# Attention scores in two matmuls instead of three and four, and a shifted order of the softmax steps on ScalarE and VectorE

## The reference

```python
# first block, heads 0-7: window of 128; 4 query heads share one of 2 key heads
s = einsum('bnqhgd,bnkhd->bnhgqk', qb, kk) * ATTN_SCALE      # then + bias, mask, softmax with a sink
# first block, heads 8-15: the two 256-token blocks, which comes to causal attention
s_own = einsum('bhqd,bhkd->bhqk', q_c, k_own) * ATTN_SCALE   # then + bias, mask, softmax
# second block, 16 heads, causal, with forget gates (F is a running sum of log_sigmoid over the tokens)
logits = einsum("bhqd,bhkd->bhqk", qb, kb) + F[q] - F[k]     # then mask, softmax
```

## Time and profile before

| | us |
|---|---|
| median of 3 runs (2031.15 to 2031.51) | 2031.24 |
| the profiled execution, device time | 2031.23 |
| its span in the profile | 2029.4 |
| first attention stage (first score at 75.8) | 73 to 245 |
| second attention stage (first score at 1406.0) | 1405 to 1591 |
| TensorE busy in the span | 1954.0 |

### The profile page before, as it was taken

One profiled execution on the slowest core, in us unless ns is written; L12 is line 12 of the kernel. 1 busy time (PEld: TensorE's weight loads), 2 busy tenths in 40 slices (PEclk: granted clock), 3 DMA queues, 4 the chain that ended last, 5 costly groups with the idle time before them and its releaser, 6 DMA issues.

```text
span 2029.4 us, 22573 instructions
## 1 busy us (share of the span) xinstructions
PE 1954.0 (96%) x9134; PEld 1607.5 (79%) x9134; DVE 1163.7 (57%) x1841; ACT 757.0 (37%) x1141; POOL 333.2 (16%) x293
## 2 busy tenths in 40 slices
PE   4999999999999999999999999999999899999997
PEld 3888888778888887887888888868888678888885
DVE  6566565576676745666655654565666554432445
ACT  4556632352223234223422122374565352222223
POOL 4422211021111102003100000147222130000002
PEclk9999999999999999999999999999999999999998
DMA  9422366266565424432654523232111122323321
GB/s 330 138 82 63 114 232 236 83 219 215 210 219 196 166 85 169 161 108 80 237 195 169 187 87 100 86 123 88 43 42 43 64 91 95 104 83 104 98 90 42
DMA packets 126121, 267.57 MB, mean 132 GB/s; under 512 B 4463, under 2 KB 33151, under 8 KB 126016
## 3 DMA queue, kind: packets, MB, share of 16 engines
q1 hardware_dynamic: 121056, 248.59, 35.9%
q0 software_dynamic: 4960, 17.53, 2.4%
HBM read 261.84 MB, written 8.45 MB: 133 GB/s over the span
## 4 chain that ended last, share of the span: by engine, by line
PE 66%; ACT 5%; DVE 4%; POOL 2%; issue 1%; DMA 1%; ACTq 0%; SPq 0%; DVEq 0%; POOLq 0%
PE ps L599 21%; PE ps L601 21%; PE ps L600 21%; DVE t L1629 1%; ACT t L1164 1%; ACT t L1160 1%; ACT t L1206 1%; ACT t L1118 1%; PE ps L756 1%; POOL t L2227 1%; DVE t L1663 1%; DVE t L1601 0%; DVE t L1554 0%; DMA x_keep<-t 0%; POOL t L2042 0%
## 5 line engine op out<-in xcount | busy, mean ns | idle before, releaser
L599 PE MATMUL ps<-t 128*128 128x512 f32 (+1 forms) x2504 | 969.5, 387 | 17.5 <-DVE t L1629 4.3
L601 PE MATMUL ps<-t 128*128 128x512 f32 (+1 forms) x2504 | 962.8, 385 | 0.0
L600 PE MATMUL ps<-t 128*128 128x512 f32 (+1 forms) x2504 | 962.0, 384 | 0.0
L599 PEld LDWEIGHTS ps<-t 128*128 128x128 f32 x2504 | 471.4, 188 | 119.0 <-DVE t L1494 6.5
L1494 DVE TENSOR_TENSOR t<-t 128x2048 fp32r<-128x2048 f32 x133 | 305.0, 2294 | 441.9 <-ACT t L1111 441.9
L601 PEld LDWEIGHTS ps<-t 128*128 128x128 f32 x2504 | 470.9, 188 | 98.9
L600 PEld LDWEIGHTS ps<-t 128*128 128x128 f32 x2504 | 471.2, 188 | 94.2 <-issue 1.0
L1111 ACT ACTIVATE t<-t 128x2048 fp32r<-128x2048 f32 x133 | 254.3, 1912 | 618.6 <-PE ps L601 611.1
L1554 DVE SCALAR_TENSOR_TENSOR t<-ps,t 128x512 f32<-128x512 f32 x184 | 132.6, 748 | 91.5 <-PE ps L601 82.7
L1506 DVE CUSTOM_DVE_ANT_0 t<-t 128x1024 f32<-128x1024 f32 x144 | 175.5, 1260 | 10.3 <-DMA t<-in_ada_t 3.6
L1629 DVE TENSOR_TENSOR t<-ps,t 64x512 fp32r<-64x512 f32 (+4 forms) x183 | 103.8, 577 | 103.4 <-ACT t L1238 48.7
(11 more groups left out here) (170 smaller groups left out, 1561.8 us busy)
## 6 DMA issues: line engine op xcount, KB each, us to landing
t<-in_ada SPq DMA_DIRECT2D x48, 1024.0 KB, 6.0
t<-in_gate SPq DMA_DIRECT2D x22, 1024.0 KB, 5.0
t<-in_up SPq DMA_DIRECT2D x22, 1024.0 KB, 5.1
t<-in_down SPq DMA_DIRECT2D x22, 1024.0 KB, 5.1
t<-in_w_in SPq DMA_DIRECT2D x17, 1024.0 KB, 5.7
t<-in_w_mlp_in SPq DMA_DIRECT2D x16, 1024.0 KB, 5.4
t<-in_w_mlp_out SPq DMA_DIRECT2D x16, 1024.0 KB, 5.1
t<-in_ada_t POOLq DMA_DIRECT2D x13, 1024.0 KB, 6.0
```

The source lines that it names most:

```text
L599: pe.matmul(o, wh, xh, start=first, stop=False)
L600: pe.matmul(o, wh, xl, start=False, stop=False)
L601: return pe.matmul(o, wl, xh, start=False, stop=last)
```

## The change

It has four parts.

1. **Scores in two matmuls.** Each head gets a full tile of 128 rows: its own 64 rows hold q-high, the other 64 hold q-low (`halves_of_queries`). The key high tile holds k-high twice, in both halves of the rows; one matmul then gives q-high by k-high and q-low by k-high. The second matmul takes the key tile with k-low in the head's own rows. In stage 1 its other rows are zero. In stage 2 they hold the ones and the forget sums (`gate_places`), and the moving side is `QF`: q-high in the head's own rows, the masked forget rows in the others. So a tile is two matmuls of the same shape in both stages, in place of three and four.
2. **Evacuation in halves.** A query tile leaves as two 64 x 512 copies on ScalarE and two 64 x 512 operations on VectorE. A key head leaves as two ScalarE copies (own rows and other rows) and one low half; the shared window keys (`ka`) with two low halves. Half of the zero memsets go (4 of 8 in stage 1 on GpSimd, 4 on VectorE and 4 on GpSimd in stage 2).
3. **Forget rows.** They are made on 32 partitions. VectorE has three more operations of 32 x 512, ScalarE three copies (one of 512, two of 1024 elements) in place of six, and GpSimd makes `QF` in two operations of 64 x 512 for each head where it had one of 128 x 512.
4. **Order.** `moved` shifts steps in an engine's own walk of the list: "score" steps are 2.5 places later on ScalarE and 2.5 sooner on VectorE, counted in the list with all engines' steps. In a causal head without evacuation VectorE now has: norm, t(h, 2), out(h-1), score 0, t(h, 3), score 1, t(h+1, 0), score 2, score 3, t(h+1, 1); ScalarE: norm, t(h, 2), out(h-1), t(h, 3), t(h+1, 0), score 0, score 1, t(h+1, 1), score 2, score 3. TensorE's and GpSimd's order stay.

The host no longer reorders the columns of `w_in` and rows of `w_branch_a`; shapes and bytes of the weight DMAs stay.

```diff
+def moved(steps, by):
+
+    return [step for _, step in sorted(enumerate(steps), key=lambda e: e[0] + by.get(e[1][0], 0))]
...
-            Qa = sb(outer, [2, 4, T], R)
-            Qb = sb(outer, [2, 4, T], R)
+            Qa = sb(outer, [8, T], R)
+            Qb = sb(outer, [8, T], R)
...
-            Q2 = sb(ph, [2, KT, T], R)
+            Q2 = sb(ph, [16, T], R)
             with ExitStack() as inner:
                 KVt = sb(inner, [12288], R)
                 pt2 = sb(inner, [2, 1280], R)
-                AFr = [sb(inner, [T], R) for _ in range(2)]
-                BF = sb(inner, [T], R)
+                QF = [sb(inner, [T], R) for _ in range(2)]
             with ExitStack() as top:
...
-                t, g = h % 4, h // 4
+                t, g = h // 2, h // 4
                 kv = KV1[0]
-                return dict(kind="swa", sink=small[:, h:h + 1], q=(Qa[:, 0, t, :], Qa[:, 1, t, :]), qt=("qa", t),
-                            k=(k_view(kv)[:, 0, g, :], k_view(kv)[:, 1, g, :]), kt=("ka", g), zero=0,
+                return dict(kind="swa", sink=small[:, h:h + 1], q=Qa[:, h, :], qt=("qa", t),
+                            out=(Qa[:, 2 * t, :], Qa[:, 2 * t + 1, :]),
+                            k=(k_view(kv)[:, 0, g, :], k_view(kv)[:, 1, 2 * g + h % 2, :]), kt=("ka", g), zero=0,
                             v=lambda j: (v_view(kv)[:, 0, j, 0:P], v_view(kv)[:, 1, j, 0:P]), vt=[("va", 0)],
-                            r0=64 * g, table=h, width=256)
+                            r0=64 * (h % 2), s0=64 * g, table=h, width=256)
             g, n = (h - 8) // 4, h % 4
...
-                if st == 1 and 4 <= h < 8:
-                    on.wait_ge(d_lo, "out", 1, h - 4)
-                if (st, hd["zero"]) == (2, 0):
-                    on.wait_ge(d_evac, "zero", 2, 0)
+                o = psum[bank][:, 0:N]
+                pe.matmul(o, hd["q"][:, tok], hd["k"][0][:, kr], start=True, stop=False)
+                q = hd["q"]
+                if st == 2:
+                    q = QF[h % 2]
+                    on.wait_ge(p_fox, "af", h)
+                    if hd["zero"]:
+                        on.wait_ge(p_fox, "bf", 1)
+                    else:
+                        on.wait_ge(a_gate, "bf", 0)
                 else:
-                    on.wait_ge(p_zero, "zero", st, hd["zero"])
-                o = psum[bank][:, 0:N]
-                pe.matmul(o, hd["q"][0][:, tok], hd["k"][0][:, kr], start=True, stop=False)
-                pe.matmul(o, hd["q"][1][:, tok], hd["k"][0][:, kr], start=False, stop=False)
-                ins = pe.matmul(o, hd["q"][0][:, tok], hd["k"][1][:, kr], start=False, stop=st == 1)
-                if st == 2:
-                    on.wait_ge(p_fox, "af", h)
-                    on.wait_ge(a_gate, "bf")
-                    ins = pe.matmul(o, AFr[h % 2][:, tok], BF[:, kr], start=False, stop=True)
-                ins.then_inc(mm.sem, mm.up("score", st, h, i))
+                    on.wait_ge(p_zero, "zero", 1, hd["zero"])
+                pe.matmul(o, q[:, tok], hd["k"][1][:, kr], start=False, stop=True).then_inc(mm.sem, mm.up("score", st, h, i))
                 freed[bank] = [(d_soft, ("top", st, h, i))]
 
...
-                on.wait_ge(a_gate, "fF")
-                on.wait_ge(d_fox, "lo")
+                on.wait_ge(d_fox, "sum rows")
...
+        own = [slice(0, 64), slice(64, 128)]
         def halves_of_keys(name, bank, i):
             kv = k_view(KV1[0] if name == "ka" else kv_of[name])
             for odd in range(2):
-                r, n = slice(64 * odd, 64 * odd + 64), 2 * i + odd
-                yield n, psum[bank][r, :], kv[r, 0, n, :], kv[r, 1, n, :]
+                n = 2 * i + odd
+                his = [kv[own[p], 0, n, :] for p in (odd, 1 - odd)]
+                if name == "ka":
+                    los = [(kv[own[p], 1, 2 * n + p, :], kv[own[p], 0, n, :]) for p in range(2)]
+                else:
+                    los = [(kv[own[odd], 1, n, :], his[0])]
+                yield n, psum[bank][own[odd], :], his, los
+        def halves_of_queries(name, t):
+            q = {"qa": Qa, "qb": Qb, "q2": Q2}[name]
+            for odd in range(2):
+                yield own[odd], q[own[odd], 2 * t + odd, :], q[own[1 - odd], 2 * t + odd, :]
...
-            for s in range(2):
-                for odd in range(2):
-                    r = slice(0, 64) if odd else slice(64, 128)
-                    yield k_view(kv)[r, s, odd::2, :].bitcast(F)
+            for odd in range(2):
+                yield k_view(kv)[own[1 - odd], 1, odd::2, :].bitcast(F)
+
+        def gate_places(kv):
+
+            for odd in range(2):
+                r = 64 * (1 - odd)
+                yield r, k_view(kv)[r:r + 32, 1, odd::2, :], k_view(kv)[r + 32:r + 64, 1, odd::2, :]
+
+        def twice(rows):
+
+            return rows.rearrange("p (a n) -> p a n", a=1).broadcast_to([32, 2, T])
...
-                act.activation(of_queries(name)[:, 0, t, :], psum[bank][:, :], ACT.Copy, scale=QSCALE).then_inc(
-                    a_hi.sem, a_hi.up(name, t))
+                for rows, hi, lo in halves_of_queries(name, t):
+                    ins = act.activation(hi, psum[bank][rows, :], ACT.Copy, scale=QSCALE)
+                ins.then_inc(a_hi.sem, a_hi.up(name, t))
 
             def keys(name, bank, n, i):
                 on.wait_ge(mm, "job", n, i)
-                for k, src, hi, lo in halves_of_keys(name, bank, i):
-                    act.activation(hi, src, ACT.Copy).then_inc(a_hi.sem, a_hi.up(name, k))
+                for k, src, his, los in halves_of_keys(name, bank, i):
+                    for hi in his:
+                        ins = act.activation(hi, src, ACT.Copy)
+                    ins.then_inc(a_hi.sem, a_hi.up(name, k))
 
...
-                for step in stage_steps[st]:
+                for step in moved(stage_steps[st], {"score": 2.5}):
...
-            act.activation(fhi[0:16, :], fr, ACT.Copy).then_inc(a_gate.sem, a_gate.up("fhi"))
-            on.wait_ge(a_gate, "fhi")
-            act.activation(fF, fhi[0:16, :].bitcast(F), ACT.Copy).then_inc(a_gate.sem, a_gate.up("fF"))
-            on.wait_ge(a_gate, "fF")
-            on.wait_ge(p_fox, "ones of AF")
-            on.wait_ge(p_fox, "ones of BF")
-            act.activation(AF[0:16, :], fF, ACT.Copy)
-            on.wait_ge(d_fox, "lo")
-            act.activation(AF[32:48, :], z3, ACT.Copy)
-            act.activation(BF[64:80, :], fF, ACT.Copy, scale=-1.0)
-            act.activation(BF[96:112, :], z3, ACT.Copy, scale=-1.0).then_inc(a_gate.sem, a_gate.up("bf"))
+            act.activation(fhi[0:32, :], fr, ACT.Copy).then_inc(a_gate.sem, a_gate.up("fhi"))
+            on.wait_ge(d_fox, "sum rows")
+            for r, one, gates in gate_places(KV2[0]):
+                ins = act.activation(gates, twice(AF[0:32, :]), ACT.Copy, scale=-1.0)
+            ins.then_inc(a_gate.sem, a_gate.up("bf", 0))
...
-                Q = of_queries(name)
                 on.wait_ge(a_hi, name, t)
-                dve.scalar_tensor_tensor(out=Q[:, 1, t, :], in0=psum[bank][:, :], scalar=QSCALE, in1=Q[:, 0, t, :].bitcast(F),
-                                         op0=ALU.mult, op1=ALU.subtract).then_inc(d_lo.sem, d_lo.up(name, t))
+                for rows, hi, lo in halves_of_queries(name, t):
+                    ins = dve.scalar_tensor_tensor(out=lo, in0=psum[bank][rows, :], scalar=QSCALE, in1=hi.bitcast(F),
+                                                   op0=ALU.mult, op1=ALU.subtract)
+                ins.then_inc(d_lo.sem, d_lo.up(name, t))
 
             def keys(name, bank, i):
-                for k, src, hi, lo in halves_of_keys(name, bank, i):
-                    low_half(lo, src, hi, name, k)
+                for k, src, his, los in halves_of_keys(name, bank, i):
+                    on.wait_ge(a_hi, name, k)
+                    for lo, hi in los:
+                        ins = dve.tensor_tensor(lo, src, hi.bitcast(F), ALU.subtract)
+                    ins.then_inc(d_lo.sem, d_lo.up(name, k))
...
-                for step in stage_steps[st]:
+                for step in moved(stage_steps[st], {"score": -2.5}):
...
-            for v in zero_places(KV2[0]):
-                ins = dve.memset(v, 0.0)
-            ins.then_inc(d_evac.sem, d_evac.up("zero", 2, 0))
...
-            dve.tensor_tensor(z3, fr, fhi[0:16, :].bitcast(F), ALU.subtract).then_inc(d_fox.sem, d_fox.up("lo"))
+            dve.tensor_tensor(z3, fr, fhi[0:32, :].bitcast(F), ALU.subtract).then_inc(d_fox.sem, d_fox.up("lo"))
+            on.wait_ge(d_fox, "lo")
+            dve.tensor_scalar(z3, z3, lower, 1.0, ALU.mult, ALU.mult).then_inc(d_fox.sem, d_fox.up("lower rows"))
+            on.wait_ge(d_fox, "lower rows")
+            on.wait_ge(p_fox, "ones of AF")
+            for r in (0, 64):
+                dve.scalar_tensor_tensor(out=AF[r:r + 32, :], in0=fhi[0:32, :].bitcast(F), scalar=upper, in1=z3, op0=ALU.mult,
```

(29 more changed lines are left out.)

86 lines of the change are left out of this document (44 added, 42 removed).

## The result

The changed kernel takes 2000.43 us (median of 4 runs) against 2031.2 us: ratio 0.9842, 95% interval 0.9828 to 0.9855, 30.8 us or 1.5% less. The prediction was 2003.3 us, range 1997 to 2012.

A forecast was written before the change was run, and what follows sets the result against it. TensorE, busy 1954.0 of 2029.4 us, was taken as the bound except in the last heads (ScalarE and VectorE). -8.9 + 1.1 - 18.1 + 0.8 - 5.0 + 2.2 = -27.9 us gave 2003.3 us, range 1997 to 2012.

The forecast's parts named there:

- A stretch where TensorE is the bound: -8.9: Stage 1: one score product fewer per tile in 8 window and 8 causal heads saves 8.9 us.
- -18.1: Stage 2 before the last heads: two of four score products go, 1.29 us a head in 14 heads.
- The last heads. Here it is the new order that counts: End of stage 2: the new order removes VectorE's two pauses, 9.6 to 7.1 us a head, saving 5.0 us.
- Rival B: Both stages: the order also removes TensorE's present idle time, 6 us more, 1994 to 1999 us; chance 0.15.
- Hidden by TensorE's projection units: Stage 1: added evacuation copies, 7.1 us of ScalarE and 2.8 of VectorE, cost nothing beside TensorE's work.
- Rival A: Middle of stage 2 or 1: softmax on ScalarE and VectorE becomes the bound, 2009 to 2018 us; chance 0.14.
- +0.8: Stage 2, three heads with a key result and four weight pieces: ScalarE's work exceeds TensorE's need, adding 0.8 us.
- +1.1: First query tiles of stage 1: four ScalarE copies delay a weight slot that TensorE waits for, by 1.1 us.
- +2.2: Start of stage 2: key copies and forget-row steps delay a weight slot TensorE needs by 2.2 us, bounds +1 and +3.5.
- C: Rival: GpSimd's added operation in each of 16 heads holds VectorE up, +11 us at most, halved 2009; chance 0.05.
- D: Rival: slower than before, VectorE standing before unmade score products while its delayed low half is needed, 2036 us; chance 0.02.
- E: Rival: the change alters nothing, because the removed score products were hidden; chance 0.01.

The follow-up runs named there:

- no_shift: The changed kernel with its two new mask columns put into unused columns of another small array, so no later array moves; 2008.7 us.
- fewer_products_new_order: The kernel before with only the new order, leaving out one score product in stage 1 and two in stage 2, evacuations as before; 1987.2 us.
- early_conversion: The changed kernel with ScalarE converting the next weight slot while it waits for the gate's sums at the start of stage 2; 1990.2 us.

## Why the prediction was right in its total and wrong in its account

Adding the medians, one part after the other, gives this account: order alone -19.5, products in the new order -24.9, evacuations and what goes with them +21.5, moved arrays -8.2; sum -31.1. The prediction had order -5.0, products -27.0, evacuations +4.1, arrays 0; sum -27.9. The steps depend on their sequence: with the products first they bring 5.6 us and not 24.9, and the order, last, 40.6.

**"A stretch where TensorE is the bound: -8.9", and "-18.1" in stage 2.** The size per product was right, 24.9 for 27.0 where TensorE does bind. The premise was wrong for the kernel before: there the omission brings 5.6. TensorE busy 165.8 of 172 us was read as bound by TensorE. But a busy share does not say that less work would end sooner: with the work removed the stage lost 0.6 us, and TensorE's idle time grew from 5.4 to 11.3. This was the step that failed first.

**"The last heads. Here it is the new order that counts", -5.0.** In the last heads it held: 6.81 and 7.57 us for 7.1. But the pause it describes, VectorE standing for ScalarE's copy behind an exponential, was in every head, and the prediction looked for it only where TensorE was visibly idle. Rival B named the place, at a chance of 0.15 and 6 us; the order is worth 19.5 alone and 40.6 with the new products.

**"Hidden by TensorE's projection units".** In stage 1 the added evacuations were costed at nothing, with a cover named by busy shares of 68 and 70%. They cost 6.8 us there, 6.5 of them ahead of the first causal head's fourth-tile exponential, so in the window heads; with the maxima alone moved 155.7 us remain against 152.6. In the old order they cost more: stage 1 is 175.3 us for the 166.5 with as many products and the old evacuations. A busy share says nothing of a queue in which each added copy lies between two handovers. Rival A's mechanism, softmax's engines as the bound, was thus at work, in stage 1, and the order kept it small. In stage 2 the +0.8 was too small as well. Of the 8.0 us there (no_shift against fewer_products_new_order) 3.2 lie ahead of the first fourth-tile exponential and 4.8 behind it; 1.1 of these are the last loop with its lower clock, and 3.7 the middle, which therefore does not hide its copies: TensorE's sums wait 5.6 us for low halves (L787) where they waited 2.2. The prediction's own sign, a softmax loop in the middle longer than 10.2 us, did come: three loops of stage 2 take 14.0 to 16.0 us. It was set badly, since the same three take 13.2 to 17.1 before and 12.9 to 14.1 without the new evacuations; over four heads of the middle the loops are 10.5 us on average for 10.1.

**First queries and start of stage 2.** +1.1 was +1.7 at the first score, and 1.4 at the wait it was read from (2.10 us where 0.74 stood). The slot at the start of stage 2 was to come 2.2 us later (2.26 by its working, which has 2.7 for VectorE in one place and adds 2.6) and came 2.3 later against the first score, so that chain was read well. But the wait at the start of stage 2 was to be 3 to 4 us and was 4.95, and the lower clock's 1.6 us behind it were in no term: the +2.2 measured 5.0: 3.4 of wait, of them 0.8 VectorE held up by GpSimd and 0.2 the two missing products, and 1.6. Of the later query tiles "hidden" was wrong for one: the forget gate's first product waits 2.92 us for VectorE (L1665), where it waited 1.55 before.

**Nothing in the sum for addresses.** The change adds two columns to a persistent array, and the text passed over them. 8.2 us, a quarter of the result.

**C, D, E.** C's price is refuted, while its collisions exist. D and E did not happen; but a time above the kernel before was nearer than 0.02 makes it, by another way than D's: without the order the same products end at 2041.0.

**The total.** The order brought 14.5 us more than its term, the evacuations cost 17.4 more, the products brought 2.1 less, and the moved arrays gave 8.2: four errors that come to 3.2 us. That the total lies in the range is luck.

## What to carry to other kernels

A nearly full engine is not a bound until less work on it shortens the stage: hold its idle time against what is to be saved, and follow two in-order engines that feed each other through one unit of the steady state, looking for "stands for the other" on both sides. Put the producer's step (here the maximum) ahead of anything in its queue that waits for the consumer; half of a reordering may do, and each stage can want its own. Judge a half by what its waits do to the engine that should be the bound, not by the idle time of the engine that you moved. Time a change of layout against a control in which only the addresses move.

## What the runs showed of the hardware that was not expected

Moving SBUF arrays by 8 or by 32 bytes a partition made the same kernel 9.0 and 10.1 us faster of 2031: where one triple of 512-column products in two took 0.70 us (0.2333 each), moved ones mostly take 0.69 or 0.68. Taking the 8 bytes back cost 8.2 us. The Trainium skill ("SBUF — State Buffer", section "SBUF: two separate sides") says that within the engine side only the port pair shared by VectorE and GpSimd causes contention and that TensorE waits for nobody; no run here shows what slows TensorE's products, but their pace does depend on addresses.

A wait of TensorE of 4.95 us was followed by 3.8 us at the lower clock, 1.6 more than at full pace, so the wait cost about 6.5 us.

VectorE and GpSimd held each other up in single operations. A 128x2048 subtraction of VectorE took 3.13 us for 2.29 when one of GpSimd had started 0.05 us ahead of it, and in early_conversion, where VectorE's started 0.10 us ahead, it kept its 2.29 and GpSimd's copy of 64x512 took 2.66 us for 0.61:

```profile
1392.82 2.66 POOL L2145 CAST t<-t 64x512 fp32r<-64x512 f32 x1 [6.03 <-DVE t L2035]
```

The same section of the Trainium skill calls the shared pair an exclusive lock, for which the one that comes later blocks fully. These rows agree: GpSimd's copy ends 0.47 us after VectorE's subtraction does. VectorE's total hides it (99.5 us busy of 146 with GpSimd's copies, 99.6 without).
